# Second attention of a three-mixture model: the heads' decay is spread over the partitions by a store and two broadcast loads, not by matmuls and copies

## The reference, cut to what matters

```
def forgetting_attention(q, k, v, log_f):          # q, k, v: (1, 512, 8, 64); log_f: (1, 512, 8)
    c = jnp.cumsum(log_f, axis=1).transpose(0, 2, 1)      # decay: one row of 512 per head
    ...
    def one_block(args):                                  # blocks of 128 queries
        logits = jnp.einsum('bqhd,bkhd->bhqk', qb, k) * scale
        decay = cb[..., :, None] - c[..., None, :]
        causal = k_pos[None, :] <= q_pos[:, None]
        logits = jnp.where(causal, logits + decay, -1e30)
        p = jax.nn.softmax(logits, axis=-1)
        return jnp.einsum('bhqk,bkhd->bqhd', p, v)
# in second_block:
z = rmsnorm(x, mix_norm) @ w_in
q, k, v, f_logit, gate_in, rec_in = jnp.split(z, ...)
log_f = log_sigmoid(f_logit + b_forget)
att = forgetting_attention(q, k, v, log_f)
rec = rg_lru(causal_depthwise_conv(rec_in, conv_w, conv_b), ...)
x = x + concat([att, rec * gelu(gate_in)]) @ w_out
```

## Time and profile before

| | |
|---|---|
| median of 3 runs | 2077.38 us |
| lowest and highest run | 2074.16 and 2081.77 us |
| span of the profiled execution (first to last instruction) | 2074.0 us |
| PE busy | 1971.6 us (95%) |
| DVE, ACT, POOL busy | 691.6, 404.9, 151.7 us |
| DMA | 596.87 MB, mean 288 GB/s |

### The profile page before, as it was taken

One profiled execution on the slowest core, in us unless ns is written; L12 is line 12 of the kernel. 1 busy time (PEld: TensorE's weight loads), 2 busy tenths in 40 slices (PEclk: granted clock), 3 DMA queues, 4 the chain that ended last, 5 costly groups with the idle time before them and its releaser, 6 DMA issues.

```text
span 2074.0 us, 25525 instructions
## 1 busy us (share of the span) xinstructions
PE 1971.6 (95%) x10045; PEld 1050.5 (51%) x10045; DVE 691.6 (33%) x1669; ACT 404.9 (20%) x874; POOL 151.7 (7%) x205
## 2 busy tenths in 40 slices
PE   8999889999999999999999999999799999999887
PEld 4444446554545453746554545454554445765443
DVE  0155657311111112635321111112738233632214
ACT  1133433111111111112111111111223322122212
POOL 0111101000000000000100000000010001211100
PEclk9999999999999999999999999999999999999999
DMA  9711104999999999823899999999941111799995
GB/s 334 215 46 47 45 24 166 414 419 420 420 421 420 421 420 378 314 64 102 332 419 420 421 421 420 421 420 417 340 118 41 41 41 33 262 380 419 420 419 216
DMA packets 127026, 596.87 MB, mean 288 GB/s; under 512 B 17489, under 2 KB 46049, under 8 KB 64095
## 3 DMA queue, kind: packets, MB, share of 16 engines
q1 hardware_dynamic: 111567, 568.06, 68.9%
q0 software_dynamic: 15376, 27.68, 4.0%
HBM read 573.48 MB, written 37.01 MB: 294 GB/s over the span
## 4 chain that ended last, share of the span: by engine, by line
PE 81%; DMA 13%; DVE 3%; ACT 2%; issue 1%; SPq 0%; DVEq 0%; ACTq 0%
PE bank L1021 22%; PE bank L679 10%; PE bank L1063 10%; PE bank L930 10%; DMA ring<-in_w_up_dram 7%; DMA ring<-in_moe_w_up_dram 6%; PE bank L826 5%; PE bank L693 4%; PE bank L665 3%; PE bank L1194 1%; PE bank L778 1%; PE bank L755 1%; PE bank L1155 1%; PE bank L921 1%; PE bank L742 1%; PE bank L712 1%
## 5 line engine op out<-in xcount | busy, mean ns | idle before, releaser
L1021 PE MATMUL bank<-ring,work 128*64 128x512 f32 (+1 forms) x2976 | 559.0, 527 | 28.0 <-DMA ring<-in_w_up_dram 24.2
L1021 PEld LDWEIGHTS bank<-ring,work 128*64 128x64 f32 x2976 | 222.7, 138 | 360.2 <-issue 335.5
L1063 PE MATMUL bank<-ring,work 128*64 128x512 f32 x1280 | 295.8, 600 | 3.9 <-DVE work L1894 3.9
L1894 DVE COPY work<-bank 128x256 f32<-128x256 f32 (+1 forms) x96 | 36.5, 380 | 693.8 <-PE bank L922 693.8
L930 PE MATMUL bank<-work 128*128 128x128 f32 x2048 | 245.7, 278 | 0.0
L930 PEld LDWEIGHTS bank<-work 128*128 128x128 f32 x2048 | 233.5, 192 | 6.1 <-issue 2.0
L679 PE MATMUL bank<-hT,ring 128*128 128x512 f32 x512 | 234.2, 599 | 0.7 <-ACT work L1257 0.7
L1353 ACT ACTIVATE work<-bank 64x512 f32<-64x512 f32 x96 | 56.7, 590 | 540.8 <-PE bank L1063 540.8
L1063 PEld LDWEIGHTS bank<-ring,work 128*64 128x64 f32 x1280 | 84.2, 136 | 144.0 <-issue 129.1
L679 PEld LDWEIGHTS bank<-hT,ring 128*128 128x128 f32 x512 | 92.4, 191 | 104.6 <-issue 102.6
L1341 ACT ACTIVATE work<-bank 64x512 f32<-64x512 f32 (+1 forms) x96 | 49.8, 518 | 476.2 <-PE bank L1021 476.2
(11 more groups left out here) (314 smaller groups left out, 1717.8 us busy)
## 6 DMA issues: line engine op xcount, KB each, us to landing
ring<-in_moe_w_down_dram SPq DMA_DIRECT2D x128, 1024.0 KB, 16.3
ring<-in_moe_w_gate_dram SPq DMA_DIRECT2D x126, 1024.0 KB, 15.3
ring<-in_moe_w_up_dram SPq DMA_DIRECT2D x126, 1024.0 KB, 17.3
ring<-in_w_down_dram SPq DMA_DIRECT2D x32, 1024.0 KB, 26.3
ring<-in_w_gate_dram SPq DMA_DIRECT2D x30, 1024.0 KB, 22.1
ring<-in_w_up_dram SPq DMA_DIRECT2D x30, 1024.0 KB, 24.4
ring<-in_attn_w_qkv_dram SPq DMA_DIRECT2D x12, 1024.0 KB, 12.8
work<-y_rows SPq DMA_DIRECT2D x12, 1024.0 KB, 7.0
```

The source lines that it names most:

```text
L1021: mm = pe.matmul(GU2[s % 2][BLK * a:BLK * a + BLK, 0:F], xgT[pair % 2][:, per * kk + k, BLK * of_pair:BLK * of_pair + BLK], v[a][k], start ...
L1063: mm = pe.matmul(DN[BLK * n:BLK * n + BLK, :], hT_[:, 2 * kk + k, :], v[:, k, 512 * n:512 * n + 512], start=(kk + k == 0), stop=(2 * kk + ...
```

## The change

For the changed kernel, the decay rows go through DRAM. GpSimd waits for the scan (`b2.c`), stores `fb[0]` (8 x 512 values) in a new DRAM tensor `decay_rows`, waits for that store, and issues a broadcast load of head 0's row to 128 partitions of `ckb[0]`. It then waits for the LRU (`b2.lruT`, 4) and issues one broadcast load of the other seven rows, 3584 values for each partition, to columns 6656 to 10240. `ckb[0]` is moved to columns 17920 to 18432, which the LRU doesn't use. PE's eight decay matmuls, ACT's eight copies, and the waits of PE and DVE for them are gone; DVE waits for the broadcasts instead, in `logits2` of turns 0 and 4, after the mask and ahead of the reduce. ACT's wait for the LRU, ahead of its copies, is gone too. To free a semaphore, `par.conv` and `par.forget` become one, `par.conv_forget`: whoever waited for 128 of the first or 32 of the second now waits for 160 (ten transfers).

```diff
@@ program
+    decay_rows = nc.dram_tensor("decay_rows", (8, S), f32, kind="Internal").ap()
@@ Parameters
-                self.conv, self.wab, self.forget = sem("par_conv"), sem("par_wab"), sem("par_forget")
+                self.conv_forget, self.wab = sem("par_conv_forget"), sem("par_wab")
@@ Attention
-                self.ckp, self.ck = sem("at_ckp"), sem("at_ck")
+                self.decay_stored = sem("at_decay_stored")
+                self.decay_spread = [sem(f"at_decay_spread{i}") for i in range(2)]
@@ tiles
-        p2, ckb = [wk(16896 + 512 * i, 512) for i in range(2)], [wk(6144 + 512 * i, 512) for i in range(8)]
+        p2, ckb = [wk(16896 + 512 * i, 512) for i in range(2)], [wk(17920, 512)] + [wk(6144 + 512 * i, 512) for i in range(1, 8)]
@@ tensor
-            pe.wait_ge(par.forget, 32)
+            pe.wait_ge(par.conv_forget, 160)
...
             pe.wait_ge(b2.copied, R_QK)
-            pe.wait_ge(b2.c, 1)
-            for hh in range(8):
-                if hh >= 4:
-                    pe.wait_ge(at.ck, hh - 3)
-                pe.matmul(bank[hh % 4][:, :], ident[0:8, hh:hh + 1].to_broadcast([8, P]), fb[0],
-                          start=True, stop=True).then_inc(at.ckp, 1)
...
-                if g < 2:
-                    pe.wait_ge(at.ck, 8)
-                else:
+                if g >= 2:
                     pe.wait_ge(at.negmax, 64 + g - 1)
@@ scalar
-            act.wait_ge(par.forget, 32)
+            act.wait_ge(par.conv_forget, 160)
...
-            act.wait_ge(b2.lruT, 4)
-            for hh in range(8):
-                act.wait_ge(at.ckp, hh + 1)
-                act.activation(ckb[hh], bank[hh % 4][:, :], ACT.Copy).then_inc(at.ck, 1)
-
@@ vector
-            dve.wait_ge(par.conv, 128)
+            dve.wait_ge(par.conv_forget, 160)
...
                 link(dve.tensor_tensor(sc[:, P * qb:n], sc[:, P * qb:n], causal, ALU.subtract))
+                if g in (0, 4):
+                    dve.wait_ge(at.decay_spread[g // 4], 16)
...
-            dve.wait_ge(at.ck, 8)
             logits2(0)
@@ gpsimd (the ten parameter loads count on par.conv_forget; then, behind those of wab:)
+            pool.wait_ge(b2.c, 1)
+            pool.dma_start(decay_rows, fb[0]).then_inc(at.decay_stored, 16)
+            pool.wait_ge(at.decay_stored, 16)
+            bcast(ckb[0], decay_rows[0:1, :], at.decay_spread[0], S)
+            pool.wait_ge(b2.lruT, 4)
+            bcast(wk(6656, 7 * S), decay_rows[1:8, :].rearrange("h n -> (h n)").unsqueeze(0), at.decay_spread[1], 7 * S)
```

More of the change, by code:

```diff
@@ L2224, in _ @@
             for i in range(4):
[L2225 to L2229, removed]
+                vector(taps[:, i, :], t["conv_w_2"][0, i:i + 1, :], par.conv_forget)
+            vector(convp[:, 16:20], t["conv_b_2"], par.conv_forget)
+            vector(convp[:, 20:24], t["b_a_2"].rearrange("l n i -> l (n i)"), par.conv_forget)
+            vector(convp[:, 24:28], t["b_x_2"].rearrange("l n i -> l (n i)"), par.conv_forget)
+            vector(convp[:, 28:32], t["lru_lambda_2"], par.conv_forget)
             pool.dma_start(wf, t["w_in_2"][0][:, 1536:1544].rearrange("(k p) n -> p k n", p=P))\
-                .then_inc(par.forget, 16)
+                .then_inc(par.conv_forget, 16)
             pool.dma_start(bfg, t["b_forget_2"].rearrange("a n -> n a"), allow_slow_non_contiguous=True)\
-                .then_inc(par.forget, 16)
+                .then_inc(par.conv_forget, 16)
             for a, n in enumerate(("w_a_2", "w_x_2")):
```

## The result

Four runs of the changed kernel have a median of 2068.31 us (2065.08 to 2069.71), four of the kernel before 2078.60 (2074.16 to 2081.77). The ratio is 0.9946 with a 95% interval of 0.9928 to 0.9963. Two later controls gave 0.9949 (0.9934 to 0.9964) and 0.9938 (0.9921 to 0.9955). The prediction was 2066.7 and 10.7 us less. Its chances were put on either side of 0.5%, 10.4 us: all three ratios lie on the far side, but each interval reaches across it.

A forecast was written before the change was run, and what follows sets the result against it. PE was taken to bound the kernel, through an unbroken PE-ACT-PE chain before scores 0. 9.73 + 1.68 - 0.68 = 10.73 us saved; from the median, 2077.4 - 10.7 = 2066.7 us, range 2061.5 to 2074.

The forecast's parts named there:

- The path: Last projection to scores 0: without decay matmuls and copies, scores 0 wait only for projected copies, 9.73 us earlier.
- The clock's part in the loop: Scores 0 to scores 2: full clock instead of half, 4.09 us instead of 5.77, so 1.68 less.
- What is late next: First transposes of the loop: DVE's first logits, then ACT's exp, make PE wait, taking back 0.68 us.
- The covers: Store and first broadcast hidden behind DVE's LRU work, second broadcast behind turns before 4: cost 0.
- Second broadcast: Heads 1 to 7, needed at DVE's reduce of turn 4: 7.3 us of 12.8 available, cost 0.
- The merged wait: DVE's LRU preparation waits for all ten parameter transfers: 0.6 us later, between 0 and 3.2, hidden by 22.08 idle.
- Rival 1: Attention loop's opening: clock falls anyway, about 10.1 us at 1.2 GHz; gain 6.1, time 2071.3; chance 10%.
- The loop's other dip: Granted clock elsewhere in the attention loop: a dip of 2.0 us that may vanish, counted in the range's lower end.
- Rival 2: DVE's reduce of turn 4: second broadcast late, slower beyond 23.5 us, at worst 2084.4; chance 10%, half for slower.
- Rival 3: Expert mixture: weight loads bound from a point PE doesn't set, gain lost, time 2077.4; chance 7%.
- Around the span: Whole execution: time outside the profiled span of 2074.0 us, bounded to about 0.2 by the fastest run, 2074.16.

The follow-up runs named there:

- controls: The changed kernel run again without edit, twice: 2069.38 us, ratio 0.9949 to the kernel before, and 2068.64 us, ratio 0.9938.
- Unpaced 8-row matmuls: Changed kernel with eight decay matmuls, 8 rows deep, put back before scores 0, results unused, without ACT's copies; one run, 2081.24 us.
- paced 128-row form: Changed kernel with eight unused matmuls, 128 rows deep, before scores 0, plus ACT's eight copies and PE's waits for them; one run, 2074.98 us.
- The late issue: Changed kernel with the second broadcast issued only after DVE's logits of turn 3, instead of at the LRU's end; 2075.86 us, ratio 0.9980 to before.
- unpaced 128-row form: Changed kernel with eight unused matmuls, 128 rows deep, put back before scores 0, without ACT's copies; one run, 2072.11 us.

## Why the prediction was right

- **The path.** It said that PE, ACT and PE form one unbroken chain from the last projection to scores 0, and that removing it moves scores 0 by 9.73 us. Measured 10.48 - 0.75 = 9.73.
- **The clock's part in the loop.** It said 1.68 us for the half clock on the opening turns, and that the fall goes with the decay matmuls. From scores 0 to scores 2 it now takes 4.73 us instead of 5.77; the step said 4.09 + 0.68 = 4.77. The clock stayed at 1.00. What it had only half right is the reason. It wrote of matmuls that waited for ACT's copies, quoted the Trainium skill for it and said that the trace agrees. The trace of before doesn't bear that out: PE was busy without a pause from the first decay matmul until the clock fell (only its weight loads waited for ACT, 1.5 us in all, four times), and each of ACT's last three copies waited 1.11 us for PE, as the one in the earlier trace rows. Unpaced 8-row matmuls took the clock down too. The stretch just ahead of the fall, before the change (columns as in rows 2):

```profile
1600.00:1602.00 2.00, 2.00 (x6) 0.93 (x5) 0.00 (x0) 2.00 (x4) 0.00 (x0) 1.00 0.00 0
```

  Part of the 9.73 us was therefore clock as well. Against the paced 128-row form the kernel before is 10.48 - 7.60 = 2.9 us longer up to scores 0 and 5.77 - 3.93 = 1.8 us from there to scores 2: of the 4.7 us, 1.8 lay in the loop's first turns and 2.9 in the decay matmuls. The sum didn't suffer, since it took the whole distance from the trace.
- **What is late next.** It said DVE, which would take back 0.68 us; PE's wait for exp is 0.65.
- **The covers.** Second broadcast 7.3 us forecast, 6.7 measured (6.6 and 6.8 in the controls); slack 5.5 forecast, 5.8 measured. First broadcast 3.8. For the store the lower end, 3.9 us from a 512 KB row, was no bound: 16 KB landed in 1.8. The merged wait cost DVE 0.59 us, forecast 0.6, and nothing on the path. (Its upper end is a slip: a landing after 8.7 us makes the wait 3.8 us later, not 3.2. Nothing hangs on it.)
- **Rival 1** (the clock falls anyway) is out for the opening: the granted clock is 1.00 in every 2 us from 1590 to 1622. The loop's other dip, which the lower end of the range let vanish, stayed and took 1.5 us more in this execution, so that scores 31 came 9.1 us earlier behind that copy and not 10.7.
- **Rival 2's price** was the step that the runs corrected. It put a late broadcast at one us for each us. The late issue shows that a stall long enough to take the clock down costs about 1.8 times itself there (8.5 for 4.8). By this one point, the change would have turned slower earlier than at the 23.5 us it gave, and the case was more dangerous than it was priced; no run shows where. It didn't occur.
- **Rival 3** (lost in the mixture) is out: from scores 2 to the end 461.2 to 462.4 us against 459.9 before, 1 to 2 us of difference in any pair of profiles and not 10. From scores 31 to the end, which is mostly the mixture, it took 341.2 to 342.6 us in the changed kernel and its controls against 341.5 before, though it began some 9 us sooner behind that copy. The 1 to 2 us come from the clock's dip between scores 24 and 26 and, in the second control, from the mixture. The unpaced 128-row form, whose code is the changed kernel's from scores 0 on, took 460.0 from scores 2, where it was 459.9 before.
- **Around the span.** It put 0.2 us around the profiled execution. The changed kernel's profiled run is listed with 2069.71 us beside its span of 2067.9, so it is 1.8. With as much around 2074.0 the profiled execution of before took 2075.8 and was none of the three runs. The forecast started from the median and didn't use it.

## What to carry to other kernels

When two profiles differ by less than you expect, measure from an event that both have to the next one behind the change: here that distance repeated to 0.01 us while the spans scattered by 3. Look at the granted clock around every stretch of matmuls that use few rows: their price is paid on them and on the work behind them, here nearly half of the gain. And when pricing a wait on the matmul engine, add what the clock does after it, since a stall of 4.8 us cost 8.5.

## What the runs showed of the hardware that was not expected

- Matmuls with 8 contracted rows took the clock from 2.4 to 1.2 GHz while PE was busy without a pause (unpaced form, below; the matmuls had started at 1601.75, and PE is busy 2.00 of every 2.00 us). With 128 rows and the same columns it stayed at 1.00. The Trainium skill ("TensorE: Matmul & The Clock Gate", What's actually happening) lets the gate follow how busy the PE is; these runs show that an engine busy by the profile isn't enough.
- A broadcast of 14 KB to each of 128 partitions (1792 KB) from one DRAM row of 14 KB took 6.7 us from issue to landing, and occupied GpSimd for only 0.54 us, as long as one of 2 KB to each partition (0.57). It took the same 6.7 us in the unpaced 128-row form, where VectorE stood idle for 5 us from its issue on, so VectorE's work beside it delayed nothing that shows.
- A 16 KB store from 8 partitions to DRAM landed in 1.8 us.

The stretches of the unpaced form with 8 rows (columns as in rows 2; the granted clock is the last column but two):

```profile
1604.00:1606.00 2.00, 2.00 (x6) 0.93 (x5) 0.00 (x0) 0.00 (x0) 0.54 (x1) 1.00 0.41 115
1606.00:1608.00 2.00, 2.00 (x5) 0.88 (x4) 0.00 (x0) 0.00 (x0) 0.00 (x0) 0.80 0.89 351
1608.00:1610.00 2.00, 2.00 (x3) 0.33 (x1) 0.00 (x0) 0.00 (x0) 0.00 (x0) 0.50 1.04 444
```
